# The depthwise convolution's running sum on VectorE, moved from SBUF to two PSUM banks

## The reference

```python
xn = rms_norm(h, n_mix_pre)
proj = xn @ w_in                                   # (T, 1024) @ (1024, 3072)
q, k, v, g, a, b = split(proj)                     # 512 columns each
qh, kh = rotary(q), rotary(k);  vh = v             # 4 heads of 128
o = retention_chunkwise(qh, kh, vh)                # chunks of 128 tokens
ret_out = head_norm(o) * silu(g)
u = a * sigmoid(b)                                 # GLU, 512 channels
y[t, c] = conv_b[c] + sum(u[t - 30 + w, c] * conv_w[w, c] for w in range(31))
conv_out = silu(layer_norm(y))
h = h + rms_norm(concat([ret_out, conv_out]) @ w_out)
h = h + rms_norm((silu(gate) * up) @ w_ffn_out)    # gate, up = rms_norm(h) @ w_ffn_in
```

## Time and profile before

| | |
|---|---|
| median of 3 runs | 1310.75 us (1310.0 to 1311.18) |
| profiled execution, first to last instruction | 1312.1 us |
| TensorE busy | 1242.5 us (95%) |
| VectorE busy | 623.9 us (48%) |
| GpSimd busy | 339.8 us (26%) |
| ScalarE busy | 342.8 us (26%) |
| VectorE's taps, L863 (`cacc`) | 87 instructions, 162.5 us |
| mean granted TensorE clock | 0.985 of full |

### The profile page before, as it was taken

The page is one execution under the profiler, slowest core; times in us unless marked ns, Lnnn a source line. Parts: engine busy times, 40 slices in busy tenths (PEclk is TensorE's granted clock), DMA queues, the critical chain, the costliest instruction groups (busy, mean ns, idle before and its releaser), DMA issues.

```text
span 1312.1 us, 19396 instructions
## 1 busy us (share of the span) xinstructions
PE 1242.5 (95%) x7890; PEld 1221.8 (93%) x7890; DVE 623.9 (48%) x832; ACT 342.8 (26%) x564; POOL 339.8 (26%) x228
## 2 busy tenths in 40 slices
PE   4999978889999999899999999999999999999995
PEld 4999977888889899899999999999999999999995
DVE  5359999996445215734151515151414242323227
ACT  5254233332325325531111111111111212121112
POOL 3057499953002205610101010101010100000006
PEclk9999999999998999999999999999999999999998
DMA  9110111112004330222120211111121211111003
GB/s 298 53 49 25 41 32 37 44 34 67 1 1 130 109 124 17 98 65 64 33 65 32 64 32 58 38 36 60 32 64 32 64 32 55 41 34 46 0 17 130
DMA packets 96145, 73.87 MB, mean 56 GB/s; under 512 B 2298, under 2 KB 88954, under 8 KB 96090
## 3 DMA queue, kind: packets, MB, share of 16 engines
q1 hardware_dynamic: 95314, 70.46, 17.7%
q10 hardware_dynamic: 784, 2.75, 0.6%
HBM read 66.54 MB, written 7.14 MB: 56 GB/s over the span
## 4 chain that ended last, share of the span: by engine, by line
PE 75%; DVE 12%; POOL 8%; issue 3%; ACT 1%; DMA 1%; POOLq 0%; ACTq 0%; DVEq 0%
PE ps L234 23%; PE ps L236 23%; PE ps L235 23%; DVE cacc L863 6%; POOL swp L390 2%; POOL cacc L378 2%; DVE w_lo L848 2%; POOL qT L393 2%; DMA x_st<-in_x_prompt 1%; DVE u L911 1%; PE ps L1377 1%; PE ps L1344 1%; POOL kT L393 1%; PE ps L1293 1%; PE ps L1312 1%
## 5 line engine op out<-in xcount | busy, mean ns | idle before, releaser
L234 PE MATMUL ps<-xf_hi,w_hi 128*128 128x344 f32 x1056 | 337.8, 320 | 1.0 <-DVE w_lo L1071 1.0
L236 PE MATMUL ps<-xf_lo,w_hi 128*128 128x344 f32 x1056 | 338.2, 320 | 0.0
L235 PE MATMUL ps<-xf_hi,w_lo 128*128 128x344 f32 x1056 | 337.8, 320 | 0.0
L436 POOL TENSOR_TENSOR act_lo<-sg,act_hi 128x344 fp32r<-128x344 f32 x66 | 61.4, 930 | 652.1 <-ACT act_hi L746 652.1
L234 PE MATMUL ps<-xn_hi,w_hi 128*128 128x350 f32 (+1 forms) x576 | 191.9, 333 | 21.8 <-DVE rc L919 16.4
L1118 DVE TENSOR_TENSOR sg<-ps,sg 128x344 f32<-128x344 f32 x66 | 34.1, 516 | 370.8 <-PE ps L236 370.6
L234 PEld LDWEIGHTS ps<-xf_hi,w_hi 128*128 128x128 f32 x1056 | 198.6, 188 | 1.2 <-DVE w_lo L1071 1.2
L236 PEld LDWEIGHTS ps<-xf_lo,w_hi 128*128 128x128 f32 x1056 | 198.7, 188 | 0.0
L235 PEld LDWEIGHTS ps<-xf_hi,w_lo 128*128 128x128 f32 x1056 | 198.7, 188 | 0.0
L235 PE MATMUL ps<-xn_hi,w_lo 128*128 128x350 f32 (+1 forms) x576 | 188.3, 327 | 0.0
L236 PE MATMUL ps<-xn_lo,w_hi 128*128 128x350 f32 (+1 forms) x576 | 188.1, 326 | 0.0
(11 more groups left out here) (167 smaller groups left out, 1518.0 us busy)
## 6 DMA issues: line engine op xcount, KB each, us to landing
f_raw<-in_w_ffn_in SPq DMA_DIRECT2D x44, 512.0 KB, 3.9
raw<-in_w_in SPq DMA_DIRECT2D x24, 512.0 KB, 3.8
f_raw<-in_w_ffn_out SPq DMA_DIRECT2D x22, 512.0 KB, 4.2
raw<-in_w_out SPq DMA_DIRECT2D x8, 512.0 KB, 6.0
out<-o_last SPq DMA_DIRECT2D x8, 512.0 KB
x_st<-in_x_prompt SPq DMA_DIRECT2D x6, 512.0 KB, 8.7
h<-in_x_prompt SPq DMA_DIRECT2D x5, 512.0 KB, 7.6
state_sb<-in_state_ret SPq DMA_DIRECT2D x4, 512.0 KB, 6.2
```

The lines of the kernel that those rows point to most:

```text
L234: nc.tensor.matmul(out, hi, mhi, start=first, stop=False)
L235: nc.tensor.matmul(out, lo, mhi, start=False, stop=False)
L236: return nc.tensor.matmul(out, hi, mlo, start=False, stop=last)
L436: g.tensor_tensor(act_lo[:, f, c0:c0 + n], sg[:, j % 2, :], act_hi[:, f, c0:c0 + n].bitcast(F32), ALU.subtract).then_inc(s_alo, 1)
```

## The change

The running sum of `conv_tap` moves from `cacc[:, 0]` in SBUF to `tap_acc`, 1024 columns that fill PSUM banks 6 and 7. The first tap of a tile writes there, the next 29 read and write it, the last one reads it and writes over `u` in SBUF as before. The window of `u` and the tap's weight stay in SBUF. `g_job(0)`, the next to write bank 6, gets a wait for all 93 taps. No instruction is added, removed or put elsewhere in any engine's order.

```diff
         ps2 = ps[:, :, :].rearrange("p (a b) n -> p a (b n)", b=2)
+        tap_acc = ps2[:, 3, :]
...
                 if w == CW - 1:
                     dve.wait_ge(s_glu, 3 * (ct + 1))
-                    v.tensor_scalar(cacc[:, 0, :], win, cw[:, ct, w:w + 1], cw[:, ct, CW:CW + 1],
+                    v.tensor_scalar(tap_acc, win, cw[:, ct, w:w + 1], cw[:, ct, CW:CW + 1],
                                     ALU.mult, ALU.add).then_inc(s_tap, 1)
                 else:
 
-                    v.scalar_tensor_tensor(out=win if w == 0 else cacc[:, 0, :], in0=win,
-                                           scalar=cw[:, ct, w:w + 1], in1=cacc[:, 0, :],
+                    v.scalar_tensor_tensor(out=win if w == 0 else tap_acc, in0=win,
+                                           scalar=cw[:, ct, w:w + 1], in1=tap_acc,
                                            op0=ALU.mult, op1=ALU.add).then_inc(s_tap, 1)
...
                 r, (c0, n) = j % H, IN_CHUNKS[j // H]
+                if j == 0:
+                    pe.wait_ge(s_tap, TAPS)
                 if j < H:
                     pe.wait_ge(s_wlo, SLOTS + N_IN - SLOTS + r + 1)
```

## The result

| | before | after |
|---|---|---|
| median of 4 runs, taken side by side | 1310.51 us | 1276.84 us |
| ratio, with its 95% interval | | 0.9743 (0.9729 to 0.9757) |
| profiled span | 1312.1 us | 1275.6 us |
| mean granted TensorE clock | 0.985 | 0.988 |

The forecast was 1277.8 us, a gain of 33.0. By the medians the gain is 33.7 us. The spans differ by 36.5, mainly because unit 3's first bank is read at 76.49 us before and at 73.98 after.

The account below looks back on a forecast made before the run. It took TensorE's waits for VectorE, whose taps GpSimd held, as the bound. Gains of 30.4 us at the projection's end and 2.6 at kv sum to 33.0: 1310.75 - 33.0 = 1277.8 us, range 1272 to 1292.

Parts of the forecast that it names:

- What bounds the kernel: From 152 to 273 us TensorE waited 16.4 us for L919, late behind taps that GpSimd's SBUF use slowed by 0.63 us each.
- The price of a tap: All 93 taps, first ones included, take 1.31 us from start to start, no longer held by GpSimd.
- lower bound: For the 93 taps: nothing less than 1.31 us, since even alone no tap was quicker.
- rival A: Each tap's in-place sum takes two passes, 1.17 us more; time 1370; slower from 1.73 us a tap; chance 0.09.
- C: Taps are held as before because the window of u or the write goes the shared way; 1310 to 1320 us; chance 0.03.
- B: PSUM writes slow to be seen delay each next tap; 1.37 to 1.73 us a tap gives 1278 to 1311; chance 0.08.
- VectorE's and GpSimd's pace: In q and k units VectorE needs 11.4 us against TensorE's 11.53, with 15 us of reserve; GpSimd keeps up too.
- TensorE's end of the projection: Unit 19's third job is read at 268.7 us instead of 299.06, a gain of 30.4 us.
- The added wait: At g_job(0): last tap ends at 263.0 us, TensorE arrives at 268.7, so the wait costs nothing, 5.7 us to spare.
- from 1.37 us a tap on, each 0.01 us more costs 0.93 us: At g_job(0), slower taps use up the 5.7 us reserve, 0.06 us a tap, then delay TensorE.
- What came behind the last tap: At kv, two splits and L942 no longer wait behind taps; kv follows g_job(1), 2.6 us more gained.
- Downstream: Everything after kv is one chain with TensorE nearly full and moves as a block.

Follow-up runs that it names:

- tile 1 alone: Against the changed kernel, only tile 1's taps keep their sum in PSUM, tiles 2 and 3 have it in SBUF again: 1297.01 us.
- tile 3 alone: Against the changed kernel, only tile 3's taps keep their sum in PSUM, tiles 1 and 2 have it in SBUF again: 1307.09 us.

## Why the prediction was right, point by point

**What bounds the kernel.** Right. TensorE waited for L919 because VectorE's queue was full of held taps; with the taps free there is no such wait, and with GpSimd's reads gone there is none either.

**The price of a tap.** 1.31 us from start to start for the 90 of L863, as forecast (two in 2.61). The 8 ns from rows 6 were the right guide, and the 65 ns that the prediction worked out from the Trainium skill, page "VectorE: DVE Perf Modes", section on the TRN2 errata, do not show: 1290 ns median in PSUM against 1285 in SBUF. The first tap of a tile takes 1.37 us from start to start (86.65 to 88.02), 0.06 more than taken, three times. Its lower bound was misread: "even alone no tap was quicker" does not hold for L859, which took 0.80 us at 89.16 before and 0.81 to 0.82 in the run where GpSimd only writes. PSUM costs each first tap 0.5 us, 1.6 in sum, which the idle time of VectorE covered. A read and a write of the same bank in one instruction cost nothing extra, so rival A falls at its first step. C falls with the maximum of 1292 beside a working GpSimd. B would have added time in a chain of dependent taps; 1.31 us from start to start leaves no room for it.

**VectorE's and GpSimd's pace.** Right in sign, too dark in size. VectorE came to unit 8 at 131.92 us (134.4 on the clock of before) against 136.4 forecast, mainly because no L911 was held, for which 6.6 us were set down; the splits of units 6 to 21 were held by 0.57 us on average and not 0.78.

**TensorE's end of the projection.** 30.35 us measured, 30.4 forecast.

**The added wait.** Free, as forecast. The last tap ended at 261.16, which is 263.7 on the clock of before, against 263.0. But that agreement is in part luck, since two errors cancelled. The prediction counted 176.4 us of work without a gap. The trace has 177.0 us from the first split's start (84.14) to the last tap's end. In 15.5 of them VectorE waited for ScalarE's high parts and copies (6.2 before splits, 7.4 before L920, 1.9 before L912), so the work itself took 161.5, 14.9 less than counted: 6.6 for L911s that were not held, 3.4 for splits that were held less, and about 5 for neighbours that overlap. So the step "from 1.37 us a tap on, each 0.01 us more costs 0.93 us" failed: at 1.51 us a tap the time is the same. Rival A's break-even, 1.73, was too low for the same reason, and since a slower VectorE meets GpSimd less: at 1.90 the kernel is still 0.1% to 0.3% faster than before. And the price of the wait once it bites was too low, 10.2 us from last tap to kv where the runs show 11.8 (tile 1 alone) to 12.8 (tile 3 alone), because of the clock.

**What came behind the last tap.** 33.30 at kv less 30.35 at unit 19 is 2.95 us, where 2.6 was forecast, and the run with kv not behind the last taps shows the same 2.95. The forecast term was kv's distance from g_job(1) alone, 2.63; the other 0.3 is g_job(1)'s own distance from unit 19, 10.17 us before and 9.89 after, which the prediction took as fixed.

**Downstream.** It moved as a block: in the 248 us from kv on TensorE was busy 238.4 us, and in 312 to 560 us before 237.7. From kv to the end it is 999.5 us after and 1000.2 before.

## What to carry to other kernels

Where VectorE and GpSimd both work through SBUF for long, look for VectorE operations with two SBUF inputs whose durations have two values (here 1.3 and up to 3.4 us). If one input can live in PSUM, the `scalar_tensor_tensor` costs the same there (1.290 us against 1.285) and neither engine is held, while a `tensor_scalar` that wrote SBUF in 0.80 us takes 1.34 into PSUM; the gain is then read at the engine that waits for VectorE, not at VectorE, and ends where that engine is full. Whoever takes PSUM banks for it takes on a wait at the next user of the banks: put its price at the wait plus the matmuls that follow at the lower clock, and work out what reserve there is from the idle time of the slowed engine, not from its sum of work alone.

## What the runs showed of the hardware that was not expected

- Memsets by GpSimd, 47.8 us of them in the stretch of the taps and splits, held neither: no tap above 1.287 us, no split above 1.227. Only its reading operations did (its arithmetic was taken away with its reads in that run).
- A `tensor_scalar` over 1024 elements took 0.80 to 0.82 us from SBUF to SBUF when it was not held and 1.34 us into PSUM. With its one input in SBUF and its output in SBUF it was still held beside GpSimd's additions, to 2.40 us before and to 2.94 in the run of tile 1; into PSUM never (1.35 at most).
- VectorE reading and writing the same two PSUM banks in one `scalar_tensor_tensor` over 1024 elements takes 1.290 us, against 1.285 us in SBUF.
- A stop of 6 us on TensorE brought a granted clock of 0.57 over the following 6.7 us, so the stop cost about 8.6 us in all (12.8 in place of 10.2 us from the last tap to kv).
- Freeing tile 2's taps shortened tile 3's stretch too, from 62.9 to 58.9 us, since GpSimd then finished sooner.
